# Wide key products, sums on VectorE, and a value pass in two halves, in the expert stage of a hybrid retention, RWKV and PEER block

## The reference

```
q = tok @ w_q ; s1, s2 = q . keys_1, q . keys_2          # 8 heads, 128 keys each
v1, i1, v2, i2 = top_k(s1, 16), top_k(s2, 16)
top, idx = top_k(v1 + v2 over all 256 pairs, 16)          # 16 experts of 16384 per head and token
gates = softmax(top)
act = gelu(ue . x) * gates          # ue: rows of expert_u
out = sum over chosen experts of act * (rows of expert_v)
```

## Time and profile before

| | us |
|---|---|
| median of 3 runs | 2376.08 (2372.18 to 2376.28) |
| profiled execution | 2374.39 |
| its span | 2372.6 |
| TensorE busy in it | 2338.8 (99%) |
| VectorE, ScalarE, GpSimd busy | 1526.2, 1340.8, 830.7 |
| U stage on TensorE (first to last line 867 product) | 928.4 to 1670.4 |
| V stage on TensorE (first to last line 923 product) | 1672.0 to 2359.8 |

### The profile page before, as it was taken

One profiled execution on the slowest core, in us unless ns is written; L12 is line 12 of the kernel. 1 busy time (PEld: TensorE's weight loads), 2 busy tenths in 40 slices (PEclk: granted clock), 3 DMA queues, 4 the chain that ended last, 5 costly groups with the idle time before them and its releaser, 6 DMA issues.

```text
span 2372.6 us, 51129 instructions
## 1 busy us (share of the span) xinstructions
PE 2338.8 (99%) x19066; PEld 2203.6 (93%) x19066; DVE 1526.2 (64%) x2468; ACT 1340.8 (57%) x2369; POOL 830.7 (35%) x612
## 2 busy tenths in 40 slices
PE   9999999999999999999999999999999999999998
PEld 8888787978888789999999999999999999999998
DVE  5568988557566565675667877776456566666534
ACT  5456554255544545777776666666555555555555
POOL 0000201100000002445556545554556566666554
PEclk9999999999999999999999999999999999999999
DMA  7665554046666557666778766675777777777684
GB/s 215 186 195 151 160 168 152 22 128 193 194 195 215 169 182 230 193 199 220 240 260 283 255 216 233 227 242 165 259 252 248 266 248 256 260 256 262 226 256 147
DMA packets 197218, 499.52 MB, mean 211 GB/s; under 512 B 14726, under 2 KB 82824, under 8 KB 187656
## 3 DMA queue, kind: packets, MB, share of 16 engines
q1 hardware_dynamic: 187719, 430.20, 57.1%
q0 software_dynamic: 9408, 68.16, 8.2%
HBM read 491.98 MB, written 5.24 MB: 210 GB/s over the span
## 4 chain that ended last, share of the span: by engine, by line
PE 92%; DVE 3%; ACT 2%; DMA 1%; POOL 1%; issue 1%; SPq 0%; ACTq 0%
PE PS L920 19%; PE PS L923 10%; PE PS L518 9%; PE PS L867 9%; PE PS L868 9%; PE PS L871 9%; PE PS L561 5%; PE PS L563 5%; PE PS L562 5%; PE PS L520 4%; PE PS L511 3%; PE PS L879 2%; DVE w_lo L1437 1%; POOL big L1364 1%; DMA raw<-in_w_out 0%
## 5 line engine op out<-in xcount | busy, mean ns | idle before, releaser
L958 ACT ACTIVATE w_hi<-raw 128x512 fp32r<-128x512 f32 x1576 | 985.6, 631 | 919.9 <-PE PS L923 291.3
L1437 DVE TENSOR_TENSOR w_lo<-raw,w_hi 128x512 fp32r<-128x512 f32 x1064 | 748.3, 715 | 759.1 <-ACT w_hi L958 757.1
L1392 POOL TENSOR_TENSOR w_lo<-raw,w_hi 128x512 fp32r<-128x512 f32 x512 | 707.7, 1392 | 1095.4 <-ACT w_hi L958 1089.3
L920 PE MATMUL PS<-act_both,w_hi 128*128 128x224 f32 x4096 | 540.5, 274 | 0.0
L920 PEld LDWEIGHTS PS<-act_both,w_hi 128*128 128x128 f32 x4096 | 498.5, 192 | 0.2 <-DVE act_both L2083 0.2
L867 PE MATMUL PS<-act_both,w_hi 128*128 128x224 f32 x2048 | 489.0, 277 | 3.6 <-ACT big L1239 3.6
L868 PE MATMUL PS<-act_both,w_hi 128*128 128x224 f32 x2048 | 483.2, 274 | 0.0
L867 PEld LDWEIGHTS PS<-act_both,w_hi 128*128 128x128 f32 x2048 | 393.0, 192 | 4.3 <-issue 4.3
L868 PEld LDWEIGHTS PS<-act_both,w_hi 128*128 128x128 f32 x2048 | 393.1, 192 | 0.0
L518 PE MATMUL PS<-act_both,w_hi 128*128 128x512 f32 x1056 | 373.2, 400 | 6.9 <-DVE w_lo L1437 6.1
L923 PE MATMUL PS<-act_both,w_lo 128*128 128x224 f32 x2048 | 312.1, 275 | 0.3 <-POOL w_lo L1392 0.2
(11 more groups left out here) (261 smaller groups left out, 1930.6 us busy)
## 6 DMA issues: line engine op xcount, KB each, us to landing
raw<-in_peer_u_t SPq DMA_DIRECT2D x256, 512.0 KB, 4.3
raw<-in_peer_v SPq DMA_DIRECT2D x256, 512.0 KB, 4.7
raw<-in_w_in SPq DMA_DIRECT2D x180, 512.0 KB, 3.8
raw<-in_w_out SPq DMA_DIRECT2D x32, 512.0 KB, 4.5
raw<-in_peer_w_q SPq DMA_DIRECT2D x32, 512.0 KB, 4.3
raw<-in_w_ret_branch SPq DMA_DIRECT2D x16, 512.0 KB, 4.4
raw<-in_w_rwkv_branch SPq DMA_DIRECT2D x16, 512.0 KB, 4.5
big<-in_x SPq DMA_DIRECT2D x2, 1024.0 KB, 5.9
```

Source lines behind the costliest of these rows:

```text
L920: pe.matmul(v_bank(j), w_hi[:, k % 2, cols], act2[:, b, w, :], start=first and j % 2 == 0 and w == 0, stop=False)
L958: act.activation(w_hi[:, slot % 2, hh * 512:(hh + 1) * 512], raw[:, slot, hh * 512:(hh + 1) * 512], ACT.Copy).then_inc(S["unit_hi"], 1)
L1392: pool.tensor_tensor(w_lo[:, k % 2, cols], raw[:, k, cols], w_hi[:, k % 2, cols].bitcast(f32), ALU.subtract).then_inc(S["p_split"], 1)
L1437: dve.tensor_tensor(w_lo[:, slot % 2, cols], raw[:, slot, cols], w_hi[:, slot % 2, cols].bitcast(f32), ALU.subtract).then_inc(S[done], 1)
```

## The change

- **Products.** The two products that share `w_hi` weights become one of 448 columns: the moving operand is the high tokens and the low tokens side by side, and the two results stand side by side in the bank. `w_lo` products stay at 224 columns and add to the first 224. So a half is four products of 448 and four of 224 in place of twelve of 224.
- **Sums in U.** The two parts of a block are added by a VectorE reduction from PSUM into G or `late_out` (`usum`); Gelu then runs in place in SBUF. The bank is freed by `usum`.
- **Low parts in U.** GpSimd makes those of units 0, 2, 3, VectorE those of unit 1.
- **V in two passes.** A bank now holds one tile of 448 columns, so eight tiles fit, and V runs over all 128 blocks twice, each time with 1024 of the 2048 channels. A unit is one block's 1024 channels, and four blocks are a pass of the loop. The rows of G are split in high and low twice. Between the passes the eight banks are emptied: the even ones summed by VectorE, the odd ones copied by ScalarE to `odd_tiles` and summed by GpSimd. At the end VectorE sums all eight.
- **Last units.** `last_units` goes by tile over the last two units, so that tiles finish one after another; `turn_rows` for the first half's channels runs between them.
- **Sparse tokens and stores.** Tiles of 224 tokens are turned alone; x1 is loaded and the output stored with tokens 0 to 31 in the last rows, by some more, smaller DMAs. Places in the passes (`MAC_AT`, `ADD_AT`, `FINAL_AT`) are set anew.

```diff
-U_SPLIT = {"p_split": (0, 2), "d_split": (1, 3)}
+U_SPLIT = {"p_split": (0, 2, 3), "d_split": (1,)}
-MAC_AT = [66 + 8 * t // 5 for t in range(PICK_TILES)]
+MAC_AT = [66 + 8 * t // 5 for t in range(17)] + [100 + 5 * t // 4 for t in range(PICK_TILES - 17)]
...
 def um(it, k):
...
-                        wait_past(pe, S[f"gelu{k // 2}"], it)
+                        wait_past(pe, S[f"gelu{k // 2}"], 2 * it - 1)
...
-                        pe.matmul(out, w_hi[:, k % 2, cols], act_hi[:, kc, SPARSE:TOK], start=kc == 0, stop=False)
-                        pe.matmul(out, w_hi[:, k % 2, cols], act_lo[:, kc, SPARSE:TOK], start=False, stop=False)
+                        pe.matmul(pair_bank(bank), w_hi[:, k % 2, cols], act_both[:, kc, :, SPARSE:TOK], start=kc == 0, stop=False)
...
 def vm(h, it, k, first=False):
+                pe.wait_ge(S["act2_split"], it * 4 + (h * BLOCKS + k + 1))
...
-                        for w in range(2):
-                            pe.matmul(v_bank(j), w_hi[:, k % 2, cols], act2[:, b, w, :], start=first and j % 2 == 0 and w == 0, stop=False)
+                        pe.matmul(pair_bank(j), w_hi[:, k % 2, cols], act2[:, k], start=first, stop=False)
...
 def gelu(it, b):
-                act.wait_ge(S["half_used"], it * 8 + (2 * U0 + 4 * b + 4))
+                act.wait_ge(S[f"gelu{b}"], 2 * it + 1)
+                act.activation(dst, dst, ACT.Gelu).then_inc(S[f"gelu{b}"], 1)
...
+            def usum(it, b, late=True):
+                dve.wait_ge(S["half_used"], it * 8 + (2 * U0 + 4 * b + 4))
+                dve.tensor_reduce(late_out[b] if late else G[:, 2 * it + b, :], summed(4 + b), AX.X, ALU.add).then_inc(S[f"gelu{b}"], 1)
...
 def gate_turn(i):
                 for par in range(2):
+                    usum(i + (GATE_AT - 1), par, not first)
...
 def u_step(unit):
                 if k % 2:
                     sparse_step(it, k // 2)
+                if unit >= 4 and k % 2 == 0:
+                    usum(it - 1, k // 2, False)
...
+            def sum_tile(h, j):
+                dve.wait_ge(S["tile_done"], 8 * h + j + 1)
+                dve.tensor_reduce(out_T[h][:, j, :], summed(j), AX.X, ALU.add).then_inc(S["out_even"], 1)
...
+            def v_lo(h, it):
+                for k in range(4):
+                    dve.wait_ge(S["act2_hi"], it * 4 + (h * BLOCKS + k + 1))
+                    dve.tensor_tensor(act2[:, k, 1, :], rowof(4 * it + k), act2[:, k, 0, :].bitcast(f32), ALU.subtract)
...
+            def last_units(h):
+                for j in range(8):
+                    for k in (2, 3):
+                        pe.matmul(pair_bank(j), w_hi[:, k % 2, cols], act2[:, k], start=False, stop=False)
+                    for k in (2, 3):
+                        last = pe.matmul(PS[:, j, 0:DT], w_lo[:, k % 2, cols], act2[:, k, 0, :], start=False, stop=k == 3)
+                    last.then_inc(S["tile_done"], 1)
+                    if h == 1 and j in (2, 4, 6):
+                        turn_rows((j - 2) // 2)
...
+                if g == 97:
+                    for j in (1, 3, 5, 7):
+                        pool.tensor_tensor(out_T[0][:, j, :], odd_tiles[:, j // 2, 0, :], odd_tiles[:, j // 2, 1, :], ALU.add)
...
-            for q in range(4):
-                even_out(2 * q)
+            for j in range(8):
+                sum_tile(1, j)
+                if j in (4, 6):
+                    for tt in range(2):
+                        add_last(tt, (j - 4) // 2)
```

More of the change, by code:

```diff
@@ L909, in vm @@
+            def vm(h, it, k, first=False):
+                pe.wait_ge(S["act2_split"], it * 4 + (h * BLOCKS + k + 1))
                 for hh in range(2):
-                    tiles = [(8 * (k % 2) + 4 * hh + t, slice((4 * hh + t) * P, (4 * hh + t + 1) * P)) for t in range(4)]
-                    pe.wait_ge(S["unit_hi"], it * 8 + (2 * V0 + 2 * k + hh + 1))
+                    tiles = [(4 * hh + t, slice((4 * hh + t) * P, (4 * hh + t + 1) * P)) for t in range(4)]
+                    pe.wait_ge(S["unit_hi"], it * 8 + (2 * (V0 + h * BLOCKS) + 2 * k + hh + 1))
@@ L921, in vm @@
-                    pe.wait_ge(*split_done("v", it, k, hh + 1))
-                    for j, cols in tiles:
-                        last = pe.matmul(v_bank(j), w_lo[:, k % 2, cols], act2[:, b, 0, :], start=False, stop=final and j % 2 == 1)
-                        if final and j % 2:
-                            last.then_inc(S["tile_done"], 1)
-                    if not final:
-                        last.then_inc(S["half_used"], 1)
-                    elif 2 * (k % 2) + hh > 0:
-                        turn_rows(2 * (k % 2) + hh - 1)
@@ L931, in turn_rows @@
-            def turn_rows(q):
-                pe.wait_ge(S["out_even"], q + 1)
-                pe.wait_ge(S["out_odd"], q + 1)
-                for tt in range(2):
+                        if first:
+                            bank_free(h, j)
+                        pe.matmul(pair_bank(j), w_hi[:, k % 2, cols], act2[:, k], start=first, stop=False)
+                    pe.wait_ge(*split_done("v", it + h * (BLOCKS // 4), k, hh + 1))
+                    for j, cols in tiles:
+                        last = pe.matmul(PS[:, j, 0:DT], w_lo[:, k % 2, cols], act2[:, k, 0, :], start=False, stop=False)
@@ L950, in _, with v_blocks @@
+            for h in range(2):
+                def v_blocks(it, first=False, final=False):
+                    for k in range(2 if final else 4):
+                        vm(h, it, k, first and k == 0)
+                    if final:
+                        last_units(h)
+                v_blocks(0, first=True)
+                with pe.Fori(1, BLOCKS // 4 - 1) as it:
+                    v_blocks(it)
+                v_blocks(BLOCKS // 4 - 1, final=True)
         @block.scalar
@@ L2096, in v_lo @@
[L2096 to L2097 removed]
+                    if k % 2:
+                        sparse_step(g, k // 2)
             dve.wait_ge(*split_done("u", UPAIRS - 1, 3, 2))
[L2099 to L2104 removed]
+            for h in range(2):
+                for it in range(BLOCKS // 4):
+                    v_lo(h, it)
```

234 lines of the change are left out of this document (131 added, 103 removed).

## The result

| | us |
|---|---|
| before, median of 10 runs | 2374.42 (2371.75 to 2376.35) |
| after, median of 10 runs | 2384.39 (2375.99 to 2388.4) |
| ratio, 95% interval | 1.0037 (1.0024 to 1.0050) |
| predicted | 2295 (2272 to 2330), faster with 0.94 |

The change makes the kernel 0.4% slower. It was forecast 80 us faster. The profiled execution of after is its fastest, 2375.99 us with a span of 2374.2; before has 2372.6.

The account below looks back on a forecast made before the run. TensorE, busy 99% of the span, was taken as the bound. From 2374.4 us, 91 came off for its pace and 13 in delays were added: 2296.4, less overlaps 2294, plus 1.7 for the median: 2295 us, range 2272 to 2330.

Parts of the forecast that it names:

- TensorE's pace, 1024 halves: U and V: a half goes from 1340 to 1251 ns, saving 91 us, with ends of 59 and 117.
- U before the gate turns: GpSimd, VectorE: U: GpSimd's low-part bursts and gathers cost 3 us, longer search portions in VectorE's queue 2 us.
- Then usum: 4.1, wanted at 5.0: U's plain passes: behind low parts, a dot and a search portion, VectorE's sum is done 0.9 us before TensorE needs the bank.
- I take 3 us for this, with 0 and 15 as ends: Gate turns: VectorE uses 11.0 of 11.8 us, 12.0 if its low parts are held up as well; cost 3 us.
- the lock: VectorE instructions with two SBUF inputs and GpSimd ones reading SBUF exclude each other for the whole instruction; reason for room upwards.
- the one thing here that gets worse: Gate turns: late_in, 0.38 or 1.42 us, takes its long form oftener as GpSimd is in low parts four fifths of the time.
- rival 2: U and V: VectorE and GpSimd hold each other up, 20 to 45 us more, 2315 to 2340; chance 0.21.
- the fifth rival: A wide product costs two narrow ones: nothing saved, 9 us added, 2385; chance 0.02.
- the fourth: TensorE stands at each block's first product until VectorE reaches usum; at 0.8 us for each of 128 blocks 2396; chance 0.03.
- The prediction's own sign of being wrong: Wide products carry more than 22 ns, or TensorE's idle time in U and V grows by over 30 us.
- the rival of the two-run operand: U's operand of two separated runs streams slower: U gains nothing, V its 45 us, 2340; chance 0.04.
- the cheaper surcharge: Wide and narrow products both carry only 13.3 ns above their columns: 26 us more saved, 2270; chance 0.10.

Follow-up runs that it names:

- e6: The changed kernel with ScalarE's Gelus one unit later in U, in gate turns also behind the one-hot scaling; 2322.85 us, 0.9780 of before.
- e11: The changed kernel with Gelus one unit later, but each 448-column product again two of 224, in U and V; 2385.47 us, 1.0042 of before.
- e9: The changed kernel with Gelus one unit later, V's additions of gathered rows spaced evenly and end additions begun after tile 2; 2320.12 us, 0.9764 of before.
- e4: The changed kernel with the sparse tokens' dot products cut from 1024 to 16 columns; 2330.92 us, 0.9820 of before.
- e5: The changed kernel with sums first, low parts two and two, V's gathered-row additions spaced evenly, end additions from tile 2; 2326.1 us, 0.9787 of before.

## Why the prediction was wrong

The sum of the prediction, before its allowance for overlaps, comes to a span of 2294.6; the trace of after has 2374.2, 80 more. By terms, in us:

| term | predicted | measured |
|---|---|---|
| TensorE's pace, 1024 halves | -91 | -77 |
| U before the gate turns: GpSimd, VectorE | +5 | +27 |
| gate turns | +3 | +41 |
| V, and between its passes | +3 | +11 |
| end | +2 | +1.3 |
| start | 0 | -2.0 |

**The step that failed** is that on VectorE in U, in both places where it is priced: for the plain passes "Then usum: 4.1, wanted at 5.0", with "Portions that are longer than the mean cost some tenths: 2 us in all", and for the gate turns "I take 3 us for this, with 0 and 15 as ends", which measured 41. Three things in it were off.
- What is behind the wait. "Behind usum are unit 1's low parts and ScalarE's Gelu" was written down and given no price. ScalarE's queue wasn't followed one instruction further, to the roundings, on which GpSimd, VectorE and TensorE all live. e6, which moves only ScalarE's work, shows what this link is worth: 61.5 us of the median, 56 in the U of the profiled executions.
- The price of a gate turn. The worst case given for a turn was 12.0 to 12.5 us, and it measured 13.4 on average: VectorE's own time isn't the bound, the ring is, and e6 has 11.9 with the lock in place. And `late_in`, called "the one thing here that gets worse", doesn't: its two forms have means of 600 and 374 ns in after, of 645 and 657 before (928 to 1640 us).
- The durations. The low part of unit 1 was to be "done at 1.4" and a dot product to take 1.22. Beside GpSimd's low parts they take 1311 ns each and up to 2.30 us. The lock was known: the paragraph on gate turns priced "If the low parts of VectorE are held up as well, it is 12.0" and rival 2 named it. But in the sum of the plain passes VectorE was given durations of before, when GpSimd was idle 175 of 372 us and the low parts of the two engines seldom lay together. The timeline of after shows both prices in one gate turn:

```profile
1409.07 0.69 DVE L1489 TENSOR_TENSOR w_lo<-raw,w_hi 128x512 fp32r<-128x512 f32 x1 [2.61 <-ACT w_hi L994]
...
1409.98 2.52 POOL L1438 TENSOR_TENSOR w_lo<-raw,w_hi 128x512 fp32r<-128x512 f32 x2
...
1410.33 2.73 DVE L1489 TENSOR_TENSOR w_lo<-raw,w_hi 128x512 fp32r<-128x512 f32 x1 [0.56 <-ACT w_hi L994]
...
1412.98 0.61 DVE L2031 TENSOR_REDUCE extra<-PS 128x224 f32<-128x448 f32 x1
...
1413.63 0.39 ACT L1281 ACTIVATE extra<-extra 128x224 f32<-128x224 f32 x1 [3.34 <-DVE extra L2031]
```

The first low part runs alone, 0.69. The second is issued 0.35 us behind the first of two GpSimd parts and ends 0.6 us after both: here it didn't get in between the two. It isn't always so. Of the pair at 1238.21, shown above, the second part begins at 1240.14, in the first of two GpSimd parts, and ends at 1241.92, while the second GpSimd part is drawn out to 1.74 us.

**Rivals.** By its time alone the outcome, 2384, is that of the fifth rival, "a wide product costs two narrow ones" (2385, chance 0.02). That is a coincidence: with the pace at 1.265 us its mechanism isn't there. Of the mechanisms, the fourth, "the sum as a new wait" (2396, chance 0.03), names the place: TensorE does wait for `usum`, but for 21 us only, and nearly all before the gate turns, not at each of 128 blocks. The second (0.21, 2315 to 2340) names the lock, which lengthens what stands ahead of the sum. Neither has the way round through ScalarE's roundings, on which most of the loss hangs. The argument against the fourth, "in-order work behind a wait shifts along with TensorE", fails because the work behind ScalarE's wait feeds what stands ahead of the next sum. The second's price was "0.5 to 1 us in each of 40 to 60 passes", of which 60 passes at 1 us would be 60 and not the 45 given as its upper end; U shows 68 us over 64 passes, about 1 a pass. The prediction's own sign of being wrong came true: TensorE's idle time in the three windows grew by 48 us, where 30 was the limit it had set.

**The pace** was of the right mechanism and mis-sized by 14 us: 75 ns a half, not 89. e11 shows that the width makes the pace: 1.34 without it. The upper end given, 1281, holds 1265. By the timeline four wide products take 0.83 us (207 ns each, 20 above their columns) and four narrow ones 0.44 (109, 16 above). On average that is (1265 - 1120) / 8 = 18.1 ns a product, the 18.3 of the earlier trace rows again and not the 16.4 of the earlier trace rows. So the surcharge didn't get cheaper; the gain is that a half has four products fewer, 4 x 18.3 = 73 of the 75 ns. (The lower end of the saving should be 60 and not 59, and the last step of the sum 2296 and not 2295; neither matters here.) Both stages have this pace (U 1.265; V 1.26), so the rival of the two-run operand is out, and so is the cheaper surcharge.

**V.** It was forecast to be 42 us shorter with its terms and is 27.5. Seven of the missing 15 are the pace. 5.9 are waits for the row's difference (line 2151, 5 times), a part of the 2 us that had ends of 0 and 12. Between the passes nothing is lost: TensorE's tiles of 448 and 224 follow each other every 0.62 to 0.63 us without idle time, for which 1 us had been set.

**The end.** The last addition comes 12.3 us after the start of the last four halves, 11.3 forecast and 10.2 before. The timeline of after, first and last of them:

```profile
2351.17 0.58 PE L961 MATMUL PS<-act_both,w_hi 128*128 128x448 f32 x2
...
2353.84 1.10 PE L948 MATMUL PS<-cst 128*128 128x128 f32 x8 [0.48 <-DVE big L2142]
...
2361.00 2.47 DVE L2179 TENSOR_TENSOR big<-big,PS 128x512 f32<-128x512 f32 x4
2361.14 1.09 PE L948 MATMUL PS<-cst,big 128*128 128x128 f32 x8 [0.72 <-DVE big L2142]
```

TensorE stands twice for VectorE's sums (0.48 and 0.72), not once for 0.4. The halves' gain is in it too, so it costs 1.3 us of span, within the 2 given.

**What would it have been.** With the order mended (e6) U is 716.6, 12 above its products alone, where the forecast had 8. So the prediction's sum describes e6 far better than after: its 2294.6, with the 14 of the pace, is 2309 for the span, where e6 has 2322.0, e9 2317.3 and after 2374.2.

**What stays open.** How much of the late sum is the lock and how much the queue's length wasn't separated: e4 shortens the queue and also what the lock can stretch. Of V's remaining 5 to 10 us no run took the differences out. The 9.5 us of e11 against before are split by stage, not by cause. And the 8.4 us between the profiled execution of after and its median have no cause shown.

## What to carry to other kernels

When an edit puts a wait in an in-order queue, follow that queue past the waiting instruction until you come to work that the awaited engine itself depends on; if there is some, the wait is a link of a ring, and its price isn't its own length. The wait that such a ring makes can show far from its cause: in the gate turns TensorE hardly waited for `usum`, but for low parts and scaled rows. Put such a wait behind the work that feeds the others, even where that makes the waiting result later: here one unit later on ScalarE gave back 61.5 us. And when work is moved to GpSimd, price VectorE's two-input instructions beside it by a row where GpSimd is busy and not by their mean in the old trace: here a dot product took up to 1.9 times and a low part up to 5 times (3.59 us) what it takes alone.

## What the runs showed of the hardware that was not expected

**The clock falls after a short idle, sometimes.** The granted clock of TensorE stands at 1.00 almost throughout, and yet in after there is this (windows, columns as above):

```profile
1262.00:1268.00 6.00, 6.00 (x39) 5.40 (x38) 4.04 (x3) 3.71 (x6) 5.71 (x5) 1.00 0.92 339
1268.00:1271.00 3.00, 0.31 (x3) 0.12 (x2) 2.79 (x4) 0.00 (x0) 0.42 (x1) 0.97 0.85 269
1271.00:1274.00 3.00, 2.94 (x10) 2.73 (x11) 2.85 (x5) 2.92 (x5) 1.96 (x2) 0.50 0.26 101
```

TensorE was busy in all of the first window, idle for 2.75 us at a late `usum`, and then worked at 0.50, the 1.2 GHz level, for about 3 us; the timeline has four wide products at nearly twice their 0.99 us just there:

```profile
1271.06 1.86 PE L876 MATMUL PS<-act_both,w_hi 128*128 128x448 f32 x4 [2.75 <-DVE big L2031]
```

That adds about 1.5 us to a wait of 2.75. The idle time of 1.86 us ahead of 1244.82, shown above, left the clock at 1.00 (its group took 1.08 us), while one of 1.85 us in e5's V was followed, one group later, by a group of 1.72 at a clock of 0.50, and one of 1.86 us in e6, at a late `usum` as well, likewise. So a wait of that length may or may not cost more than itself. The ten runs of after fit this in part: the six with a mean granted clock of 0.994 or less took 2383.2 to 2388.4 us, and of the four at 0.995 or more three took 2376.0 to 2379.3 and one 2384.5. So some of the spread between its runs may come from the clock; it wasn't tried.

**A wide product carries more than a narrow one.** 20 ns above its columns for 448, some 16 for 224 behind it, 18.3 for 224 among its like the earlier trace rows, and 13.3 for 512 alone. What sets this was not looked into.
